# Keeping the rows of the last pair of experts on chip and adding them by products with a turned one-hot table

## The reference, cut to what matters

```python
top_p, top_i = lax.top_k(jax.nn.softmax(e_logits, axis=-1), TOP_K)          # 2 of the 8 experts of one group
weights = g_gate[:, None] * top_p / jnp.sum(top_p, axis=-1, keepdims=True)
expert = g_idx[:, None] * EXPERTS_PER_GROUP + top_i                          # 32 experts in all
comb = jnp.einsum('tk,tke->te', weights, jax.nn.one_hot(expert, N_EXPERTS, dtype=jnp.float32)).astype(h.dtype)
a = jnp.einsum('td,edf->tef', h, w_g)
u = jnp.einsum('td,edf->tef', h, w_u)
return jnp.einsum('tef,efd->td', jax.nn.silu(a) * u * comb[:, :, None], w_d)
# and in the layer:  x = x + hmoe(rmsnorm(x, g_ffn[layer]), ...)
```

## Time and profile before

| | us |
|---|---|
| time, median of 3 runs | 1447.49 (1433.95 to 1448.58) |
| the profiled execution | 1442.71 |
| its span | 1440.8 |
| last pair of layer 0, from its gate/up products to the next block | 615.3 to 639.7 |
| first block of `layer_b`, to its third projection chunk | 639.7 to 666.9 |
| last pair of layer 1 to the end | 1399.7 to 1440.8 |

### The profile page before, as it was taken

One profiled execution on the slowest core, in us unless ns is written; L12 is line 12 of the kernel. 1 busy time (PEld: TensorE's weight loads), 2 busy tenths in 40 slices (PEclk: granted clock), 3 DMA queues, 4 the chain that ended last, 5 costly groups with the idle time before them and its releaser, 6 DMA issues. The chain is left out here.

```text
span 1440.8 us, 20756 instructions
## 1 busy us (share of the span) xinstructions
PE 1304.7 (91%) x8642; PEld 925.8 (64%) x8642; DVE 625.2 (43%) x940; ACT 323.9 (22%) x642; POOL 440.0 (31%) x381
## 2 busy tenths in 40 slices
PE   7899999999899978879999999999999889997782
PEld 5678888645666645536868868868756646664451
DVE  2277675623412211125448658558436542221114
ACT  3222232312122211202005115005005312221110
POOL 4122325100011111002986667577540101111100
PEclk9999999998699999999999999999999979999996
DMA  9944534273689999992322222122051779999995
GB/s 337 310 122 146 163 101 147 75 304 125 247 351 418 418 420 419 421 312 56 91 53 53 55 53 72 29 53 92 9 132 22 306 277 418 418 418 421 420 397 199
DMA packets 154865, 319.90 MB, mean 222 GB/s; under 512 B 63061, under 2 KB 112101, under 8 KB 130069
## 3 DMA queue, kind: packets, MB, share of 16 engines
q1 hardware_dynamic: 139764, 280.47, 52.2%
q0 software_dynamic: 13824, 33.84, 6.5%
q10 hardware_dynamic: 1184, 4.26, 0.8%
HBM read 300.71 MB, written 34.33 MB: 233 GB/s over the span
## 5 line engine op out<-in xcount | busy, mean ns | idle before, releaser
L1719 PE MATMUL ps<-slots 128*128 128x384 f32 x768 | 261.9, 495 | 0.6 <-ACT slots L1917 0.2
L1719 PEld LDWEIGHTS ps<-slots 128*128 128x128 f32 x768 | 203.6, 270 | 43.7 <-issue 3.5
L1021 PE MATMUL ps<-slots,oT 128*64 128x256 f32 x1536 | 180.0, 390 | 32.7 <-DMA slots<-in_w_up 31.3
L1021 PEld LDWEIGHTS ps<-slots,oT 128*64 128x64 f32 x1536 | 125.5, 140 | 93.6 <-issue 35.6
L575 PE MATMUL ps<-xnT_a,wA 128*128 128x260 f32 (+1 forms) x768 | 174.0, 387 | 3.4 <-DMA wA<-in_w_qkv_a 2.6
L575 PEld LDWEIGHTS ps<-xnT_a,wA 128*128 128x128 f32 x768 | 146.5, 192 | 28.9 <-issue 4.5
L1456 POOL DMA_INDIRECT y_rows<-ysb,idx x32 | 32.1, 1003 | 405.6 <-DVE ysb L1056 405.6
L1047 DVE TENSOR_TENSOR h<-sg,ps 64x256 f32<-64x256 f32 x64 | 26.4, 413 | 263.2 <-ACT sg L1044 260.0
L1039 PE MATMUL ps<-slots,hT 128*64 128x512 f32 x384 | 87.7, 597 | 2.3
L1056 DVE COPY ysb<-ps 64x512 f32<-64x512 f32 x64 | 44.4, 694 | 88.2 <-PE ps L1039 88.2
L1044 ACT ACTIVATE sg<-ps 64x256 f32<-64x256 f32 x64 | 24.3, 380 | 246.8 <-PE ps L1021 238.2
(11 more groups left out here) (277 smaller groups left out, 1994.8 us busy)
## 6 DMA issues: line engine op xcount, KB each, us to landing
slots<-in_w_down SPq DMA_DIRECT2D x48, 1024.0 KB, 21.4
slots<-in_w_gate SPq DMA_DIRECT2D x48, 1024.0 KB, 25.7
slots<-in_w_up SPq DMA_DIRECT2D x48, 1024.0 KB, 29.2
wA<-in_w_qkv_a SPq DMA_DIRECT2D x24, 512.0 KB, 4.5
slots<-in_w_q_b SPq DMA_DIRECT2D x12, 1024.0 KB, 7.6
spare<-in_w_gate SPq DMA_DIRECT2D x8, 1024.0 KB, 16.5
spare<-in_w_up SPq DMA_DIRECT2D x8, 1024.0 KB, 19.2
gain_rows<-in_w_gate SPq DMA_DIRECT2D x8, 1024.0 KB, 20.6
```

Source lines behind the costliest of these rows:

```text
L1021: last = nc.tensor.matmul(bank(q)[lo:lo + CAP, 0:FE], x[:, k, :], wt[:, k, :], start=(k == 0), stop=(k == KT - 1))
L1719: last = nc.tensor.matmul(bank(i % 2)[:, 0:UW], xT[:, kt, cols], wB[:, g, kt, :], start=(kt == 0), stop=(kt == KT - 1))
```

## The change

- VectorE, in both layers, after `over_i`: the tokens whose rows fit into the first 64 places (`fits`) are told from the others; `share` holds the weight of a token for expert 30 and 31; `wts` becomes zero where a token's row is one of the last pair's (or beyond 64), `wts_far` keeps the weights of the rows beyond 64. `sel[t]` (128 tokens x 128 places of the last pair) is the one-hot of the place times that weight, made by two products and a sum of 128x640.
- TensorE, in the last pair, turns the five tiles of `sel` in place of a next pair's rows; ScalarE copies them to `sel_T`. The last pair's y goes to `y_last`, also in SBUF, and is not scattered.
- The sync queue and ScalarE's queue wait for the scatters of pairs 0 to 14 and ask for the y rows within the expert block: ScalarE between its last silu and its last two copies, the sync queue behind unit 0's loads. Units 1 and 2 go to the start of `layer_b`.
- `last_pair`: two products of `sel_T` and `y_last` for each tile, left in PSUM, give the sum of the last pair's rows with their weights. Two of them replace fillers in `layer_b`; the others lie between turns and projections. Fillers go from 5 to 2 products at the end of the experts and from 7 to 2 in `layer_b`.
- `layer_b`: `add_back` of tile 0 comes ahead of `scale(0, 0)`, and has a third instruction that adds the product from PSUM.
- Last block: ScalarE multiplies the second row by its weight, GpSimd adds x, VectorE adds the first row times its weight to the product, and the two sums.
- The path for rows beyond 64 uses other places and adds its rows itself (not shown).

```diff
+        yr = slots[:, 0:ARENA].rearrange("p (k n) -> p k n", n=D)
+        y_last, sel_T = flat(oT)[:, 2 * D:3 * D], flat(oT)[:, 3 * D:3 * D + TOK]
+        def rows_back(eng, layer, k):
+            for t, rows in TILES:
+                r0 = TOK * k + 128 * t
+                eng.dma_start(yr[0:rows, 2 * t + k, :], y_rows[r0:r0 + rows, :]).then_inc(s_back[layer][t], 16)
+        def last_pair(t, rows, b, sig):
+            for n in range(2):
+                last = nc.tensor.matmul(bank(b + n)[0:rows, :], sel_T[:, 128 * t:128 * t + rows], y_last[:, 512 * n:512 * n + 512],
+                                        start=True, stop=True)
+            last.then_inc(sig, 1)
...
@@ moe, sync @@
-                        for g in range(NDIL):
-                            for n in unit_pieces(g):
-                                used(n)
-                            load_unit(sp, 0, g)
+                        for n in unit_pieces(0):
+                            used(n)
+                        load_unit(sp, 0, 0)
+                    for i in range(ARENA // PIECE):
+                        used(PIECES - RING + HOME.index(i))
+                    all_stored(sp)
+                    rows_back(sp, layer, 0)
...
@@ moe, tensor, experts(v) @@
-                        if v < NE // 2 - 1:
+                        if v < LAST:
                             pe.wait_ge(s_xs[1 - b], 16 * (n + b) + 16)
                             for half in range(2):
                                 turn_half(pe, 1 - b, half, s_xt)
+                        else:
+                            pe.wait_ge(s_sel, 1)
+                            for t, rows in TILES:
+                                last = nc.tensor.transpose(bank(2 + t // 4)[:, 128 * (t % 4):128 * (t % 4) + rows],
+                                                           sel[0:rows, t].rearrange("p q c -> p (q c)"), ident[0:rows, 0:rows])
+                            last.then_inc(s_selt, 1)
...
-                        keep_busy(5, 2)
+                        keep_busy(2, 0)
...
@@ moe, scalar, experts, last pair @@
+                        else:
+                            act.wait_ge(s_selt, 1)
+                            nc.scalar.activation(sel_T[:, 0:SEQ], bank(2), ACT.Copy)
+                            nc.scalar.activation(sel_T[:, SEQ:TOK], bank(3)[:, 0:DEC], ACT.Copy)
+                            all_stored(act)
+                            rows_back(act, layer, 1)
...
@@ moe, vector, after over_i @@
+                    fits, others = (flat(kept[:, n]) for n in range(2))
+                    dve_do(V.tensor_scalar(fits, place[:, :], float(CAP), None, ALU.is_lt))
+                    dve_do(V.tensor_tensor(kept[:, 1], oh[:, 0:2, :, NE - 2], oh[:, 0:2, :, NE - 1], ALU.add))
+                    dve_do(V.tensor_scalar(others, others, -1.0, 1.0, ALU.mult, ALU.add))
+                    dve_do(V.tensor_tensor(others, others, fits, ALU.mult))
+                    dve_do(V.tensor_scalar(fits, fits, -1.0, 1.0, ALU.mult, ALU.add))
+                    V.tensor_tensor(wts_far[:, :, :], wts[:, :, :], kept[:, 0], ALU.mult)
+                    dve_do(V.tensor_tensor(share[:, :, :, :], oh[:, 0:2, :, NE - 2:NE], wts[:, :, :].unsqueeze(3).to_broadcast([128, 2, NT, 2]), ALU.mult))
+                    dve_do(V.tensor_tensor(wts[:, :, :], wts[:, :, :], kept[:, 1], ALU.mult))
...
+                    for k in range(2):
+                        ins = V.tensor_tensor(picks[k], at[:, NT * k:NT * k + NT, :].unsqueeze(2).to_broadcast([128, NT, 2, CAP]),
+                                              share[:, k].unsqueeze(3).to_broadcast([128, NT, 2, CAP]), ALU.mult)
+                    dve_do(ins)
+                    V.tensor_tensor(picks[0], picks[0], picks[1], ALU.add).then_inc(s_sel, 1)
...
@@ moe, gpsimd @@
-                        scatter(v)
+                        if v < LAST:
+                            scatter(v)
...
@@ last block @@
+                        last_pair(t, rows, BANK[t], s_lp)
...
+                        pool.wait_ge(s_far, t + 1)
+                        far = yr[0:rows, 2 * t + 1, :]
+                        nc.gpsimd.tensor_tensor(far, far, x[0:rows, t, :], ALU.add).then_inc(s_add, 1)
...
+                        act.wait_ge(s_back[layer][t], 32)
+                        far = yr[0:rows, 2 * t + 1, :]
+                        nc.scalar.activation(far, far, ACT.Copy, scale=wts[0:rows, 1, t:t + 1]).then_inc(s_far, 1)
...
+                        dve.wait_ge(s_lp, t + 1)
+                        V.scalar_tensor_tensor(out=near, in0=near, scalar=wts[0:rows, 0, t:t + 1], in1=bank(BANK[t], 2)[0:rows, :],
+                                               op0=ALU.mult, op1=ALU.add).then_inc(s_near, 1)
+                        dve.wait_ge(s_near, t + 1)
+                        dve.wait_ge(s_add, t + 1)
+                        V.tensor_tensor(xt, near, far, ALU.add).then_inc(s_cb, 1)
...
@@ layer_b, sync @@
-                    rows_back(sp, 0)
+                    load_unit(sp, 0, 1)
+                    load_unit(sp, 0, 2)
...
@@ layer_b, tensor @@
-                    keep_busy(6, 0)
+                    last_pair(*TILES[0], PROD_BANK[0], s_lp)
+                    last_pair(*TILES[1], PROD_BANK[1], s_lp)
+                    keep_busy(2, 6)
                     turn_x(*TILES[0])
-                    keep_busy(1, 0)
+                    last_pair(*TILES[2], PROD_BANK[2], s_lp)
                     project(0, 0, 0)
                     turn_x(*TILES[1])
+                    pe.wait_ge(s_xc, 1)
+                    last_pair(*TILES[3], PROD_BANK[3], s_lp)
                     turn_x(*TILES[2])
                     project(0, 0, 1)
                     turn_x(*TILES[3])
+                    pe.wait_ge(s_xc, 2)
+                    last_pair(*TILES[4], PROD_BANK[4], s_lp)
                     turn_x(*TILES[4])
...
@@ layer_b, vector, add_back and its calls @@
+                        dve.wait_ge(s_lp, t + 1)
+                        V.tensor_tensor(xt, xt, bank(PROD_BANK[t], 2)[0:rows, :], ALU.add).then_inc(s_cb, 1)
...
+                    add_back(*TILES[0])
                     dve.wait_ge(s_gcol, 32)
                     scale(0, 0)
-                    for t, rows in TILES:
+                    for t, rows in TILES[1:]:
                         add_back(t, rows)
```

More of the change, by code:

```diff
@@ L348, in unit_pieces, with rows_of_layer @@
             return [3 * NE - RING + HOME.index(i) for i in range(lo // PIECE, -(-hi // PIECE))]
+        yr = slots[:, 0:ARENA].rearrange("p (k n) -> p k n", n=D)
+        y_last, sel_T = flat(oT)[:, 2 * D:3 * D], flat(oT)[:, 3 * D:3 * D + TOK]
+        s_back = []
+        def rows_of_layer(layer):
+            s_back.append([nc.alloc_semaphore(name=f"y_back{t}_{layer}") for t in range(NT)])
+        def rows_back(eng, layer, k):
[7 more added lines that the diff above has]
+            last.then_inc(sig, 1)
+        rows_of_layer(0)
         phA = ExitStack()
@@ L938, in moe @@
                 ring = [home(i) for i in HOME] + [flat(spare[:, 0:2]), flat(spare[:, 2:4]), flat(gain_rows), oT_flat[:, 0:2 * D]]
-                over_w = [home(k) for k in range(3)]
+                over_w = [home(5), home(6), ring[12]]
+                over_xT = ring[13][:, 0:D].rearrange("p (k c) -> p k c", k=KT)
+                over_row = ring[13][:, D:2 * D]
+                LAST = NE // 2 - 1
                 def gate_up_of(w):
@@ L1065, in all_stored, with all_down, further_blocks @@
                     for w in range(2):
-                        eng.wait_ge(s_yo[w], 16 * ROUNDS)
+                        eng.wait_ge(s_yo[w], 16 * (ROUNDS - w))
+                def all_down(eng):
+                    all_stored(eng)
+                    for q in range(2):
+                        eng.wait_ge(s_dn[q], NE // 2)
                 @contextmanager
-                def further_blocks(eng, prologue=None, count=None):
+                def further_blocks(eng, prologue=None, count=None, epilogue=None):
                     if count is None:
@@ L1476, in _, with over_rows_free @@
                             count = over_count(pool)
-                        scatter(v)
-                    with further_blocks(pool, lambda: all_stored(pool), count) as (m, _):
+                        if v < LAST:
+                            scatter(v)
+                    def over_rows_free():
+                        all_down(pool)
+                        for s in s_back[layer]:
+                            pool.wait_ge(s, 32)
+                    with further_blocks(pool, over_rows_free, count) as (m, _):
                         def mark(n):
@@ L1579, in layer_b @@
                 junk = flat(sq)[:, 0:D]
-                s_gt = [sem(f"b_y_back{t}") for t in range(NT)]
+                PROD_BANK, TURN_BANK = (0, 2, 6, 4, 2), (4, 2, 6, 4, 2)
+                s_lp = sem("b_last_pair_done")
                 s_kvo = [sem(f"b_kv_stored{g}") for g in range(NDIL)]
@@ L1592, in layer_b @@
```

(4 more changed lines are left out.)

153 lines of the change are left out of this document (86 added, 67 removed).

## The result

The changed kernel took 1447.26 us at the median of 12 executions (1435.92 to 1450.0), the kernel before, timed beside it, 1437.02 us (12 executions, 1431.97 to 1448.58). The ratio on record is 1.0047, 95% interval 1.0024 to 1.007; it isn't the quotient of the two medians, 1.0071 (the means are 1445.66 and 1439.43, 1.0043). I had forecast 7.9 us off, so the change moved the other way, by less than the 1% that I had called the limit of what can be told. Two slow executions of the kernel before, over 1.5% above the fastest of their timing (1463.28 and 1452.32 us), are left out of the counts in experiment 8.

The account below looks back on a forecast made before the run. TensorE was busy 91% of the span, with gains only in the idle seams behind each layer's last expert pair; 4.5 us in layer 0 plus 3.4 in layer 1's tail, 7.9 off 1447.5, gave 1439.6 us, range 1428 to 1451.

Parts of the forecast that it names:

- The table: Selection table on VectorE before the first pair, both layers: 4.0 us of work, hidden behind a wait for ScalarE, cost 0.
- Rival D: VectorE's 4 us for the selection table are not hidden in either layer; nothing won, 1447.6 us; chance 0.05.
- The block change: End of layer 0's experts: next block begins at 632.6 instead of 639.7, 7.1 us earlier.
- Rival C: Layer 0: sync queue's row issues stall, block changes at 637, both seams win 4.3 us, 1443.2 us; chance 0.14.
- Tile 0's rows at 634.5: Layer 0's attention block: first tile's y rows are there at 634.5, bounds 633.6 and 640.
- rival B: Layer 0's y rows come late behind unit 0's small packets; 3.7 us slower, 1451.2 us, deciding from 642.4; chance 0.08.
- my signs of being wrong: VectorE waiting for layer 0's rows beyond 636; last block starting unshifted; both adds at free length; TensorE waiting on picks.
- From tile 0 to chunk 2: Layer 0's attention: third projection chunk comes 27.8 us behind tile 0's first add, 20.7 before.
- the 4.5: Seam behind layer 0: third projection chunk starts at 662.3 instead of 666.85, 4.5 us won.
- The tail: Layer 1's end: block change at 1416.0, VectorE and GpSimd adds excluding each other, over in 19.2 us; 3.4 us won.
- rival A: Layer 1's tail: the VectorE-GpSimd lock costs nothing, adds take 15.0 us, 12.1 off in all, 1435.4 us; chance 0.18.
- The base: The forecast was taken off 1447.5 us, the median of three runs of the kernel before, spread over 15 us.

Follow-up runs that it names:

- experiment 8: Changed kernel timed a third time, 1444.58 us, and layer 0's part alone a second time, 1445.46 us, both without fillers; executions of all timings counted.
- Experiment 4: Changed kernel with both halves of layer 0's tile 0 rows asked for by ScalarE's queue: with filler products 1430.06 us, without 1435.45 us.
- both filled kernels: Kernel before and changed kernel, each with filler products keeping TensorE at work round and in both routings: 1435.45 and 1434.96 us.
- the timing with the clock out: Layer 1's part of the change alone, with filler products in both routings: 1431.79 us, 3.7 off the filled kernel before.
- Experiment 5: Filled kernel with layer 1's part alone, VectorE's first sum left in PSUM: 1428.84 us; filled whole change with that and tile 0 on ScalarE's queue: 1425.44 us.
- the last kernel: Whole change with fillers, tile 0's rows on ScalarE's queue and VectorE's first sum left in PSUM: 1425.44 us, ratio 0.9894 to the kernel before.
- the three timings: The changed kernel unaltered and without fillers, timed three times beside the kernel before: 1447.26, 1439.48 and 1444.58 us.
- experiment 2: Filler products keep TensorE at work round and in both routings: kernel before 1435.45 us, changed kernel 1434.96 us.
- seam one alone: Layer 0's part of the change, layer 1 as in the kernel before, no fillers: 1448.64 us, ratio 1.0069; a second time 1445.46 us, ratio 1.0034.
- the tail alone: Layer 1's part of the change, layer 0's seam as in the kernel before, no fillers: 1433.51 us, ratio 0.999.
- the experiment meant for that: Filler products between layer 0's first two attention units: changed kernel with 8 1445.69 us, with 16 1448.7; kernel before with 12 1447.72.

## Why the prediction was wrong

*The table* cost nothing, as forecast. Its last instruction on VectorE starts at 396.11, and the first job of the experts, the one of the earlier trace rows, still waits 4.32 us in the changed kernel:

```profile
396.11 0.82 DVE L1450 TENSOR_TENSOR sel<-sel,who 128x640 f32<-128x640 f32 x1
401.25 0.41 DVE L1073 TENSOR_TENSOR h<-sg,ps 64x256 f32<-64x256 f32 x1 [4.32 <-ACT sg L1070]
```

The whole table took 4.0 us, from 392.95 to 396.93, the sum that I had worked out. Rival D is out.

*The block change* came at 633.2 (632.6 forecast, 639.7 before). Rival C, with a block change at 637, is out.

*Tile 0's rows at 634.5* is the step that failed in the seam: 638.2. I had named what would delay them, the sync half behind unit 0, and had its 16.02 us issue in the earlier trace rows, but took a value near the lower bound. The issue itself was about where I had it (626.6 for 626.3). The landing wasn't: I had started from the 4.9 us of the earlier trace rows, ScalarE's half took 5.1 and SyncE's 11.5. Experiment 4 shows that this was the cause: asked for on the other queue, tile 0 waits for nothing, and the seam is 4.1 us shorter. This is rival B's mechanism, short of the 642.4 us from which I let it decide the outcome, and it is the first of my signs of being wrong: VectorE waited for rows beyond 636.

*From tile 0 to chunk 2* I had 27.8 us; 28.05 were measured, and 27.3 and 28.0 with tile 0 on time, with fillers and without. So the order worked out there was right, and chunk 2's start won 0.6 us: the 4.5, less the 3.7 of the late rows. With tile 0 on time chunk 2 starts 46.8 us behind the first product of layer 0's last pair, where both filled kernels have 50.9: 4.1 of the 4.5 were there to be won.

*Chunk 2 itself* took 1.6 us longer, which my sum had at no change: the lower level of the clock at its start. It isn't this execution's accident: with the new seam it took 12.0 to 12.3 us in 13 of 14 profiles, with the old one 10.59 in all six. The waits of TensorE for tile 4's last add, 1.37 us, and for the eviction, 0.72, stand ahead of it in all 14 new ones and in none of the old ones. But they don't bring the clock down by themselves. In the one new profile that is left, that of tile 0 on ScalarE's queue without fillers, the same waits stand there and the chunk ran through at 1.00:

```profile
651.75 1.04 PE L1801 MATMUL ps<-cst,x 8*128 8x8 f32 x8 [1.37 <-DVE x L2077]
653.51 10.59 PE L1817 MATMUL ps<-slots 128*128 128x384 f32 x32 [0.72 <-DVE vo L2105]
```

No run took the waits away. Further on, the first eight product records of the next attention output took 5.37 us for 3.67 in the profile after, another 1.7; that came in six of the 14 and in one of the six.

*The tail* was right in each term: block change 0.9 us after the last copy (1.6 forecast), adds over 19.5 us (19.2), VectorE's two-SBUF add lengthened from 1.23 to 2.06 and 3.28 (forecast 2 to 3.4), 4.0 us won (3.4), and 3.7 in the timing with the clock out. Experiment 5 shows the lock as the cause, by taking one SBUF operand away: VectorE's adds went back to 1.22 us, GpSimd's from 3.0 (11.99 for four) to 2.36, and rival A's free run, 15 us, came to be 15.4 from block change to the last add in the last kernel. The Trainium skill (SBUF — State Buffer, Who interferes with whom) says that a VectorE instruction with at most one SBUF input, outside the modes that use two ports, doesn't contend with GpSimd; the trace agrees, with VectorE's add of 1.22 us at 1413.77 running into GpSimd's of 1414.00.

*What was left out* is the larger error. The sum had no term for the clock of a routing, though the profile of the kernel before held both levels of it, 21.7 and 14.2 us for the same 121 products: a swing of 7.5 us in each layer, as large as all that I forecast. With the clock out, the change is worth 0.5 us by medians; by its halves it is -3.7 + 2.3 = -1.4. Without, the three timings gave 10.2 us slower, 2.0 faster and 4.1 slower than the kernel before beside them by medians, and 6.2, 0.5 and 2.9 slower by means. The first, that of the result section, lies at the unlucky end.

*The base* was luck too, of the other kind. The 1447.5 us that I subtracted from were the median of three executions; twelve of the same kernel gave 1437.02. So 1447.26 lies inside my 1428 to 1451 by a base that was 10.5 us high. Off 1437.0 the forecast would have been 1429.1, 18 us from what was measured.

*What stays open* is why the changed kernel has both routings at the lower level more often. The profiles lie at spans of 1430.4 us with both routings at the upper level, 1440.8 with one, 1445.9 and 1446.6 with none. If executions below 1438 us are taken for the first kind, up to 1446 for the second and above for the third, the changed kernel has 8, 12 and 16 of its 36 and the kernel before 70, 82 and 17 of its 169. That makes 1.22 and 0.69 routings at the lower level for each execution, an estimate of 4.0 us between the kernels at 7.5 apiece; the means differ by 3.7, the clock's shares by 4.6. That the clock of the two routings carries most of the loss is shown by experiment 2.

The new seam doesn't fix the levels: the changed kernel's three profiles have both routings low, both high and both low, seam one alone had 13.8 and 21.8 us once and 21.9 and 21.8 the other time, and the tail alone, with the old seam, 14.0 and 21.8. One thing goes with layer 1's level in all 12 profiles in which that routing has no fillers. The attention output some 30 us ahead of it has the eight records named above. In five profiles they took 5.37 us, and the routing took 21.6 to 21.8. In the other seven they took 3.67, and the routing 13.6 to 14.5. The rows of the changed kernel and of the kernel before:

```profile
1109.55 5.37 PE L276 MATMUL ps<-slots,oT 128*128 128x512 f32 x8 [1.28 <-PEq L1655]
...
1108.60 3.67 PE L276 MATMUL ps<-slots,oT 128*128 128x512 f32 x8 [1.28 <-PEq L1552]
```

So which level the routing gets shows before it begins, with either seam. What settles it no run shows; that it hangs on the moment at which the work comes would fit, but the experiment meant for that missed its sizes. The means of the three timings (1445.7, 1440.9 and 1441.9) differ by no more than 12 executions of this spread can, so the size of the effect, some 3 to 5 us on the mean, is not settled either.

## What to carry to other kernels

Where a profile shows the same stretch once at either level of TensorE's clock, the difference belongs into the range as a term of its own, and a variant should be compared with that stretch filled, before a difference smaller than it is believed. A load that is asked for early is only as early as its place on the queue: look at what the queue is still carrying and at how long its last loads took to land, and give the first tile to the queue that is free. Three executions are no base where they lie 15 us apart. A sum of VectorE that is to run beside GpSimd should keep one operand in PSUM.

## What I had not expected of the hardware

The clock's swing decided more than the change: 121 products, with TensorE busy for 97% of the time or more, took 21.7 us or 13.7, and filler products ahead of and between them kept them at 15.1 to 16.5 and narrowed the spread of whole executions from 14 or 20 us to 7. The Trainium skill (TensorE: Matmul & The Clock Gate, What's actually happening) says that what watches TensorE's activity runs on by itself and does not start with the kernel, so that one kernel sees different clocks in different runs, and puts the cost of coming up to speed under 1% of a span. The traces agree that runs of one kernel differ, with 21.6 and 13.7 us for one routing; whether for that reason, no run here shows. The cost was up to 15.4 us of 1430, a little more than 1%.

One issue on SyncE's queue took 15.6 to 16.4 us in every one of the 20 profiles, at the same place (a small piece of unit 0's weights), while ScalarE's queue issued layer 0's rows at 0.34 to 0.78 us each in the changed kernel, and 1.33 at most in any. Rows asked for on the sync queue behind those weights took 11.5 and 12.8 us to land, rows asked for 2 us earlier on ScalarE's 5.1 and 4.4.
